# Two output tiles opened at once: the start of the second input product in a two-block kernel

## What is computed

```
x = x + rms_norm(f, norm_ffn_post)            # end of block 1: residual of the feed-forward
h = rms_norm(x, norm1_g_2)                    # start of block 2
z = h @ w_in_2                                # 1024 x 2560: the "second input product"
a, gate, q, k, v = split(z)                   # a, gate: convolution; q, k, v: attention
u = a * sigmoid(gate)                         # then a depthwise convolution with 31 taps
q, k = rms_norm per head; attention over a grid neighbourhood
x = x + concat(conv_out, attn_out) @ w_out_2
```

## Time and profile before

| | us |
|---|---|
| median of 3 runs | 1470.35 (1470.22 to 1470.82) |
| the profiled execution, its own time | 1470.5 |
| its span, from the first instruction recorded to the last | 1468.7 |
| TensorE busy in the span | 1459.0 (99%) |
| VectorE / ScalarE / GpSimd busy | 674.5 / 585.6 / 654.5 |
| the seam: first product of tile 0 starts | 888.01 |
| tile 2 starts | 907.08 |

### The profile page before, as it was taken

One profiled execution on the slowest core, in us unless ns is written; L12 is line 12 of the kernel. 1 busy time (PEld: TensorE's weight loads), 2 busy tenths in 40 slices (PEclk: granted clock), 3 DMA queues, 4 the chain that ended last, 5 costly groups with the idle time before them and its releaser, 6 DMA issues.

```text
span 1468.7 us, 19733 instructions
## 1 busy us (share of the span) xinstructions
PE 1459.0 (99%) x7128; PEld 1179.5 (80%) x7128; DVE 674.5 (46%) x1087; ACT 585.6 (40%) x922; POOL 654.5 (45%) x304
## 2 busy tenths in 40 slices
PE   9999999999999999999999999999999999999999
PEld 7888888888788878888888886777678888888887
DVE  6424755775534286333330108989764333333000
ACT  5143433756553253332232224766654332232221
POOL 4434322762244434444444452766234444444543
PEclk9999999999999999999999999999999999999999
DMA  5433211112123223333233333322122333233333
GB/s 186 147 87 89 84 58 44 58 44 58 58 87 98 89 72 102 99 100 95 90 100 101 113 101 117 112 73 70 42 77 86 100 100 95 91 100 100 100 107 123
DMA packets 38573, 134.15 MB, mean 91 GB/s; under 512 B 4496, under 2 KB 4752, under 8 KB 38512
## 3 DMA queue, kind: packets, MB, share of 16 engines
q1 hardware_dynamic: 37248, 130.70, 29.4%
q10 hardware_dynamic: 1264, 2.62, 0.6%
HBM read 131.20 MB, written 2.10 MB: 91 GB/s over the span
## 4 chain that ended last, share of the span: by engine, by line
PE 78%; issue 13%; DVE 4%; POOL 3%; ACT 0%; DMA 0%; POOLq 0%; SPq 0%; DVEq 0%
PE bank L1157 17%; PE bank L1158 17%; PE bank L1159 17%; POOL wL L483 3%; PE bank L1511 3%; PE bank L1512 2%; PE bank L1513 2%; PE bank L1186 2%; PE bank L1188 2%; PE bank L1187 2%; PE bank L1287 1%; PE bank L1288 1%; PE bank L1289 1%; DVE bank L2247 1%; PE bank L1566 1%
## 5 line engine op out<-in xcount | busy, mean ns | idle before, releaser
L483 POOL TENSOR_TENSOR wL<-raw,wH 128x1024 fp32r<-128x1024 f32 x234 | 574.8, 2457 | 759.5 <-ACT wH L579 621.2
L579 ACT ACTIVATE wH<-raw 128x1024 fp32r<-128x1024 f32 x209 | 221.3, 1059 | 587.3 <-PE bank L1159 519.3
L1157 PE MATMUL bank<-aH,wH 128*128 128x512 f32 x920 | 359.5, 391 | 0.4 <-POOL wL L483 0.3
L1159 PE MATMUL bank<-aH,wL 128*128 128x512 f32 x920 | 358.0, 389 | 0.0
L1158 PE MATMUL bank<-aL,wH 128*128 128x512 f32 x920 | 358.0, 389 | 0.0
L1157 PEld LDWEIGHTS bank<-aH,wH 128*128 128x128 f32 x920 | 172.7, 188 | 38.9 <-issue 1.0
L1159 PEld LDWEIGHTS bank<-aH,wL 128*128 128x128 f32 x920 | 172.7, 188 | 36.1
L1158 PEld LDWEIGHTS bank<-aL,wH 128*128 128x128 f32 x920 | 172.7, 188 | 35.7 <-issue 0.5
L1158 PE MATMUL bank<-fL,wH 128*128 128x512 f32 x352 | 137.0, 389 | 0.0
L1157 PE MATMUL bank<-fH,wH 128*128 128x512 f32 x352 | 137.0, 389 | 0.0
L1159 PE MATMUL bank<-fH,wL 128*128 128x512 f32 x352 | 136.9, 389 | 0.0
(11 more groups left out here) (336 smaller groups left out, 2013.2 us busy)
## 6 DMA issues: line engine op xcount, KB each, us to landing
raw<-in_w SPq DMA_DIRECT2D x234, 512.0 KB, 3.5
bmk<-in_bias SPq DMA_DIRECT2D x6, 512.0 KB, 4.8
out_x<-xT SPq DMA_DIRECT2D x8, 256.0 KB, 4.3
xT<-in_x SPq DMA_DIRECT2D x3, 512.0 KB, 7.3
ct<-in_ct ACTq DMA_DIRECT2D x3, 384.0 KB, 4.0
xT<-in_x SPq DMA_DIRECT2D x2, 256.0 KB, 3.9
raw<-in_w SPq DMA_DIRECT2D x2, 256.0 KB, 4.2
w1k<-in_w1k ACTq DMA_DIRECT2D x1, 512.0 KB, 4.0
```

What stands on the lines that cost most here:

```text
L483: pool.tensor_tensor(wL[:, c_slot, :], raw[:, c_slot, :], wH[:, c_slot, :].bitcast(F32), ALU.subtract).then_inc(sem("w_lo"), 1)
L579: act.activation(wH[:, s, :], raw[:, s, :], ACT.Copy).then_inc(sem("w_hi"), 1)
L1157: pe.matmul(bank[:], hi, H[:, ka, :], start=(k == 0), stop=False)
L1159: mm = pe.matmul(bank[:], lo, H[:, ka, :], start=False, stop=(k == p.k - 1))
```

## The change

At the seam the first two output tiles are worked on together. Five things go with it.

1. The weight stream is laid out anew (`halves_of_two`): the first chunk of `in2` holds k-blocks 0 to 3 of both tiles, the second k-blocks 4 to 7. TensorE does the high products of a k-block for tiles 0 and 1, then the sums, and the low products of k-blocks 0 to 3 in between; those of 4 to 7 come at the end.
2. The sums of squares use `token_sums`: `sq` is the weight (four blocks of 128 tokens), one column of ones the input. The result is 128 tokens x 4 columns.
3. The root is therefore made on 128x4 values (`token_root`), TensorE spreads it over bank 6 after two k-blocks of tile 2, and VectorE copies it to `nr`.
4. VectorE's low parts of k-blocks 0 to 3 lie behind the residuals 2 to 5, the other four at the end.
5. ScalarE converts the chunk of tile 2 between the high parts 5 and 6, and VectorE makes that chunk's low part, which GpSimd made before. `ffn1_done` comes after it.

```diff
@@ -548,7 +548,10 @@
                         .then_inc(sem("conv_add"), 1)
             for t in range(1, NT2 + 1):
-                low((i2 + t + 1) % 2, i2 + t + 2)
+                if t == 2:
+                    pool.wait_ge(sem("w_lo"), i2 + 3)
+                if t > 1:
+                    low((i2 + t + 1) % 2, i2 + t + 2)
                 if 4 <= t < 4 + TAPS // 2:
                     add_taps(2 * t - 7, 2)
             lows(PH["out2"].c0 + 2, NCHUNK)
@@ -949,9 +952,10 @@
             rsqrt(4, narrow(B[4]), D, (sem("sum_ready"), 4), root, narrow(B[5]))
 
-            high_of_x("h3", "g_norm1", "res2", 4, True)
-
             p = PH["in2"]
+            high_of_x("h3", "g_norm1", "res2", 4, True, range(6))
+            ahead(p, 0)
+            high_of_x("h3", "g_norm1", "res2", 4, True, range(6, KD))
             w = PV_AT["dw"] + 3 * TAPS
             def evicted(t):
@@ -1021,7 +1025,7 @@
                 act.wait_ge(sem("na_pv"), TT * (pp + 1))
                 act.activation(rows_first(mH[:, pp, :]), columns_first(B[5][:]), ACT.Copy).then_inc(sem("na_hi"), 1)
-            rsqrt(5, B[6][:], D, (sem("sum_ready"), 5), nr[:], B[5][:])
+            rsqrt(5, narrow(B[6]), D, (sem("sum_ready"), 5), root, narrow(B[5]))
             act.preload_act_table_set("sigmoid_and_others")
             for t in range(1, NT2):
                 kind, n = IN2[t - 1]
@@ -1029,7 +1033,8 @@
                     act.preload_act_table_set("sigmoid_and_others")
                 if t in SPREAD_AT:
                     head_roots_wide(SPREAD_AT[t])
-                ahead(p, t - 1)
+                if t > 1:
+                    ahead(p, t - 1)
                 if t - 1 in VALUES_AT:
                     values(VALUES_AT[t - 1], 1)
                 if kind in "gqk":
@@ -1503,8 +1508,7 @@
             def add_up(k):
                 pe.wait_ge(sem("sq_ready"), 4 * KD + k + 1)
-                pe.matmul(B[6][:], ones, sq[:, k % 2, :], start=(k == 0), stop=(k == KD - 1),
-                          skip_group_check=True).then_inc(sem("sq_used" if k < KD - 1 else "sum_ready"), 1)
+                token_sums(B[6], sq[:, k % 2, :], k == 0, k == KD - 1).then_inc(sem("sq_used" if k < KD - 1 else "sum_ready"), 1)
             def block_product(bank, s, b, H, L, start, stop):
                 hi, lo = wH[:, s, b * P:(b + 1) * P], wL[:, s, b * P:(b + 1) * P]
@@ -1597,38 +1601,39 @@
                 mm.then_inc(sem("na_pv"), 1)
 
-            bank0, bank1 = (B[(p.t0 + t) % NBANK] for t in range(2))
-            s0, s1 = (p.c0 % 2, (p.c0 + 1) % 2)
-            pe.wait_ge(sem("w_lo"), p.c0 + 1)
-            pe.wait_ge(sem("bank_free"), p.t0 + 1)
+            first_two = [B[(p.t0 + t) % NBANK] for t in range(2)]
+
+            def pair_blocks(k):
+
+                return (p.c0 + k // 4) % 2, [slice((t * 4 + k % 4) * P, (t * 4 + k % 4 + 1) * P) for t in range(2)]
+
+            def high_products(k):
+                if k % 4 == 0:
+                    pe.wait_ge(sem("w_lo"), p.c0 + k // 4 + 1)
+                pe.wait_ge(sem("h3_hi"), k + 1)
+                s, blocks_ = pair_blocks(k)
+                for t in range(2):
+                    pe.matmul(first_two[t][:], wH[:, s, blocks_[t]], aH[:, k, :], start=(k == 0), stop=False, skip_group_check=True)
+                    pe.matmul(first_two[t][:], wL[:, s, blocks_[t]], aH[:, k, :], start=False, stop=False, skip_group_check=True)
+
+            def low_products(k):
+                pe.wait_ge(sem("h3_lo"), k + 1)
+                s, blocks_ = pair_blocks(k)
+                for t in range(2):
+                    mm = pe.matmul(first_two[t][:], wH[:, s, blocks_[t]], aL[:, k, :], start=False, stop=(k == KD - 1), skip_group_check=True)
+                if k % 4 == 3:
+                    mm.then_inc(sem("chunk_done"), 1)
+
+            pe.wait_ge(sem("bank_free"), p.t0 + 2)
             for k in range(KD):
-                b = slice(k * P, (k + 1) * P)
-                pe.wait_ge(sem("h3_hi"), k + 1)
-                pe.matmul(bank0[:], wH[:, s0, b], aH[:, k, :], start=(k == 0), stop=False, skip_group_check=True)
-                pe.matmul(bank0[:], wL[:, s0, b], aH[:, k, :], start=False, stop=False, skip_group_check=True)
+                high_products(k)
                 add_up(k)
-            def low_products(ks):
-                for k in ks:
-                    pe.wait_ge(sem("h3_lo"), k + 1)
-                    mm = pe.matmul(bank0[:], wH[:, s0, k * P:(k + 1) * P], aL[:, k, :], start=False, stop=(k == KD - 1), skip_group_check=True)
-                return mm
-
-            def high_products(k):
-                b = slice(k * P, (k + 1) * P)
-                pe.matmul(bank1[:], wH[:, s1, b], aH[:, k, :], start=(k == 0), stop=False, skip_group_check=True)
-                pe.matmul(bank1[:], wL[:, s1, b], aH[:, k, :], start=False, stop=False, skip_group_check=True)
-
-            pe.wait_ge(sem("w_lo"), p.c0 + 2)
-            pe.wait_ge(sem("bank_free"), p.t0 + 2)
-            low_products(range(KD - 3))
-            for k in range(2):
-                high_products(k)
-            low_products(range(KD - 3, KD)).then_inc(sem("chunk_done"), 1)
-            for k in range(KD):
-                if k >= 2:
-                    high_products(k)
-                mm = pe.matmul(bank1[:], wH[:, s1, k * P:(k + 1) * P], aL[:, k, :], start=False, stop=(k == KD - 1), skip_group_check=True)
-            mm.then_inc(sem("chunk_done"), 1)
+                if 2 <= k < 5:
+                    low_products(k - 2)
+                if k == 4:
+                    low_products(3)
+            for k in range(4, KD):
+                low_products(k)
             for t in range(2, NT2):
                 if t >= 4:
                     pe.wait_ge(sem("bank_free"), NBANK + p.t0 + max(t - 1, 1))
@@ -1647,6 +1652,8 @@
                         pe.wait_ge(sem("ln_add"), 3)
                         pe.wait_ge(sem("conv_out"), 3)
                         pe.matmul(B[7][:], ones, ssum[:], start=True, stop=True).then_inc(sem("sum_ready"), 1)
+                    if k == 2 and t == 2:
+                        spread_root(3, B[6])
                     if k == 2 and t in SPREAD_AT:
                         head_spread(SPREAD_AT[t], 0)
                     if k == 3 and t - 1 in STEP_AT:
@@ -1674,7 +1681,7 @@
                     pe.wait_ge(sem("sq_used"), 5 * KD + 4)
                     token_sums(B[7], ssum, True, True).then_inc(sem("sum_ready"), 1)
                 if slot == 20 and b == 3:
-                    spread_root(3, B[7])
+                    spread_root(4, B[7])
                 if slot == 22 and b == 3:
                     value_turns(3, 0)
                 if slot == 23 and b == 2:
@@ -2148,7 +2155,7 @@
             clear_sum(1)
             copy_and_square(PH["out1"], zT, 1)
-            def residual_and_low(src, gain, name, use, next_gain, spread, lows_last=False):
+            def residual_and_low(src, gain, name, use, next_gain, spread, lows):
                 dve.wait_ge(sem("root_spread"), spread)
                 for kt in range(KD):
@@ -2156,13 +2163,12 @@
                         .then_inc(sem(name + "_mul"), 1)
                     dve.wait_ge(sem(name + "_mul"), kt + 1)
                     dve.tensor_tensor(xT[:, kt, :], xT[:, kt, :], tmp[:, kt % 2, :], ALU.add).then_inc(sem(name), 1)
-                    if kt and not lows_last:
-                        low_of_x(use, next_gain, kt - 1)
-                for kt in range(0 if lows_last else KD - 1, KD):
-                    low_of_x(use, next_gain, kt)
+                    for n in lows.get(kt, ()):
+                        low_of_x(use, next_gain, n)
             token_root(2, B[4], D, narrow(B[5]))
-            residual_and_low(zT, "g_mix_post", "res1", "h2", "g_ffn_pre", 1)
+            residual_and_low(zT, "g_mix_post", "res1", "h2", "g_ffn_pre", 1,
+                             {kt: (kt - 1,) if kt < KD - 1 else (kt - 1, kt) for kt in range(1, KD)})
             clear_sum(2)
             for kt in range(KD):
                 add_square(2 * KD + kt)
@@ -2200,17 +2206,23 @@
             clear_sum(3)
             copy_and_square(PH["dn1"], z2T, 3)
             token_root(4, B[4], D, narrow(B[5]))
-            residual_and_low(z2T, "g_ffn_post", "res2", "h3", "g_norm1", 2, True)
+            residual_and_low(z2T, "g_ffn_post", "res2", "h3", "g_norm1", 2,
+                             {2: (0,), 3: (1,), 4: (2,), 5: (3,), KD - 1: range(4, KD)})
+            p = PH["in2"]
+            s_ = (p.c0 + 2) % 2
+            dve.wait_ge(sem("w_hi"), p.c0 + 3)
+            dve.tensor_tensor(wL[:, s_, :], raw[:, s_, :], wH[:, s_, :].bitcast(F32), ALU.subtract).then_inc(sem("w_lo"), 1)
             dve.wait_ge(sem("res2"), KD)
             dve.sem_inc(sem("ffn1_done"), 1)
-            norm(5, B[6], B[5])
+            token_root(5, B[6], D, narrow(B[5]))
+            dve.wait_ge(sem("root_spread"), 3)
+            link(dve.tensor_copy(nr[:], B[6][:]))
```

(10 more changed lines are left out.)

## The result

| | before | changed |
|---|---|---|
| median of 12 runs, us | 1470.14 (1467.99 to 1471.52) | 1473.88 (1470.59 to 1475.38) |
| ratio, 95% interval | | 1.0024 (1.0016 to 1.0032) |
| profiled execution, its own time / span | 1470.5 / 1468.7 | 1474.35 / 1472.6 |

The account below looks back on a forecast made before the run. TensorE, busy 1459.0 of 1468.7 us, was taken as the bound, with VectorE pacing the seam. Seam -0.5, transposes +0.5 and the wait from the held copy +1.2 gave +1.2 us: 1471.6, range 1468.3 to 1474.2.

Parts of the forecast that it names:

- The seam's sum: Seam on TensorE: 18.3 us of work plus 0.2 waiting for high part 6; tile 2 starts 0.5 us earlier.
- spreading the root: Four transposes in tile 2 on TensorE, 0.49 us paid in full: +0.5 us.
- A narrow sum: Four one-column matmuls in the seam take 0.82 us to the next matmul's start, against 0.85 for a wide sum.
- The chunk on VectorE: Tile 2's chunk: its subtraction on VectorE takes 1.3 us, done at 904.3, ahead of tile 2 at 906.6; cost 0.
- The later `ffn1_done`: Behind the seam: it moves from 897.6 to 904.3; GpSimd's zeros and the load for tile 4 still fit; cost 0.
- What VectorE's later `nr` does: Tile 4: copy nrc starts about 0.4 us behind GpSimd's subtraction, is held until 916.3, done 2.6 us later than before.
- How it comes back: Second gating, taps and tile 6's chunk each move by 1.2 us, so TensorE waits 1.2 us ahead of tile 6.
- The clock: TensorE's granted clock: the summed forecast includes no added loss from it; a fall costs about 1.7 us.
- Rival C: Clock falls in the seam behind narrow sums, about 1.7 us each: 1473.3 with one, 1475 with two; chance 0.14.
- A: Rival: the copy nrc is not held and the second gating absorbs VectorE's 0.75 us; 1470.4, no change; chance 0.19.
- D: Rival: the clock fall at 1011 is not repeated, 1.7 us less, 1469.9; chance 0.12.
- B: Rival: the seam's sums are nearly free, tile 2 starts 3.0 us earlier; 1468.6, or 1467.4 without the held copy; chance 0.12.

Follow-up runs that it names:

- run 7: The changed kernel with the low part of tile 2's chunk made by GpSimd again, the copy nrc still from SBUF; ratio 1.0019 to the kernel before.
- run 1: The changed kernel with the copy nrc reading bank 6 instead of nr in SBUF; ratio 1.0003 to the kernel before, median 1470.72 us.
- run 2: The kernel before with one added VectorE pass (bank 6 to a free tile) just ahead of the copy nrc; ratio 1.0015 to the kernel before.
- run 3: The kernel before with the same added VectorE pass as run 2, but just behind the copy nrc; ratio 0.9998 to the kernel before.
- run 5: The changed kernel with wide sums and the root as before, no transposes in tile 2, two tiles still open; ratio 1.0017 to the kernel before.
- run 4: The changed kernel with two unread 512-column matmuls just ahead of TensorE's wait for tile 6's chunk; ratio 1.0009 to the kernel before, median 1471.46 us.
- run 6: Run 5 with nrc made by a second last Newton step reading one SBUF and one bank operand, not copied; ratio 1.0002 to the kernel before.
- run 8: Run 6 with ScalarE converting tile 2's chunk behind high part 7, not ahead of high part 6; ratio 0.9999 to the kernel before.
- run 10: Run 1 with every narrow sum made twice, the first into a bank nobody reads; ratio 1.0111 to the kernel before.
- run 9: Run 1 with seven of the eight sums of squares left out on TensorE; ratio 0.9980 to the kernel before, median 1467.50 us.

## Why the prediction was right, and what it had too small

*The seam's sum* was forecast as 18.6 us and measured as 18.60; *spreading the root* as 0.49 and measured as 0.48. *A narrow sum* was forecast at 0.82 us and took 905.43 - 904.62 = 0.81. The Trainium skill (TensorE: Matmul & The Clock Gate, LDWEIGHTS (loading the stationary operand)) gives 128 columns / 1.2 per load, 107 ns; eight of them would be 0.85 us, an estimate from that figure. The trace roughly agrees, with eight records in 0.81 us. The chunk on VectorE took 1.22 us and cost nothing that can be told (run 7). The later `ffn1_done` cost nothing either; GpSimd's zeros came at 902.97 in the changed kernel's profile, where I had them behind 904.3.

*What VectorE's later `nr` does*: the copy was forecast to start 0.4 us behind GpSimd and started 0.35 behind; it was held, as rows 6 and 7 hinted. That was the step on which the sign rested, and runs 1, 2 and 3 show it from three sides. The two pages of the Trainium skill that the prediction names there (VectorE: DVE Perf Modes, Mode 2×_2P, and GPSIMD Engine Reference, Key points) agree with what the traces show: 2.52 us within SBUF in the changed kernel, 0.68 from a bank in run 1.

*How it comes back* is the mis-sized term: 1.2 us forecast, 1.7 measured. I let ScalarE's taps follow the second gating at once, as they do before. But ScalarE loads a table between its sigmoid and them. Before:

```profile
920.22 1.28 ACT L963 ACT_TABLE_LOAD   x1
922.35 0.82 ACT L1053 ACTIVATE yT<-up,pv 128x512 f32<-128x512 f32 x1 [0.84 <-DVE up L2232]
```

In the changed kernel:

```profile
922.93 0.63 ACT L965 ACTIVATE pk<-pk 128x512 f32<-128x512 f32 x1 [2.89 <-DVE pk L2230]
923.58 1.28 ACT L967 ACT_TABLE_LOAD   x1
924.87 0.81 ACT L1058 ACTIVATE yT<-up,pv 128x512 f32<-128x512 f32 x1
```

Before, the load ended at 921.50 and the taps waited for the gating until 922.35. Now the gating ends at 924.28, as late as forecast (1.2 behind, without the start's 0.75), and the taps wait for the table until 924.87. When the gating got shorter than the load, the load became what is late next: 0.6 us.

*The clock* is the term that the sum put at nothing. Rival C had the mechanism and tied it to the seam. In the changed kernel's profile the clock fell behind the wait ahead of tile 6, which cost 1.4 us. That does not follow from the wait alone: of the four profiles with an idle wait of 1.8 us there, two have the fall (the changed kernel, run 2) and two have not (runs 5 and 7). The clock also fell in the seam in two of the four profiles with eight narrow sums (runs 4 and 7, not the changed kernel and run 1). Of the six profiles with wide sums (before, 2, 3, 5, 6, 8) none has a fall that starts in the seam; in run 3 one started in the window from 885, ahead of it, and reached about half a microsecond into it. Two of four against none of six is no proof that narrow sums at this density cause it; run 10, with twice the density, is strong for it.

How much of the 3.5 us is the clock can be estimated from the mean granted clocks on record. It is 0.9978 over the changed kernel's twelve executions and 0.9991 over the 83 of before that were measured beside the experiments. At the lower level a product takes 0.43 us instead of 0.23, so about half of the time there is lost, and the shares missing from 1.000, times 1470 us, are 3.3 and 1.4 us of loss: about 1.9 us more in the changed kernel. The other 1.6 us fit the +1.73 of the wait. The clocks are recorded to a thousandth, so this is rough. Which wait or which narrow work brings a fall on in a given execution stays open.

A and D did not occur in the changed kernel's profile: the copy was held, and the later fall came again, at 1015. The later fall is absent from the profiles of runs 3, 5, 7, 9 and 10, so it comes and goes whatever the change. B is refuted by runs 9 and 10. Its price of 3 us for free sums was about right: 2.4 in the trace.

So the direction and the path were right, and that the time lies within the range was partly luck. The forecast and the 0.8 us left for the rest end at 1472.4; the range reached 1474.2 only to make room for C, a fall in the seam, and it was used up by the table and by falls that came also elsewhere. The chance of 0.14 for "slower" was too small: C was tied to the seam alone, while the forecast case had a new wait of over a microsecond in it, and rows 10 and 11 had already shown a fall behind narrow work and a wait.

## What to carry to other kernels

Before moving work on VectorE by a few tenths of a microsecond, look which of its instructions read and write only SBUF and what GpSimd does at that moment. The copy here was short when it started first (0.61 us) and lasted until GpSimd was done when it started second (2.52), and reading the same values from a bank avoided it (0.68). Price a sum by a row of the trace and not by its columns: four matmuls of one column, eight records, cost 0.81 us, and one of 512 columns 0.85. And count a new wait of TensorE with the clock that it may cost: here 1.8 us of waiting had a fall of the clock behind it in two profiles of four, worth 1.4 us more in the changed kernel's.

## What was not expected of the hardware

- The holding is one-sided. A copy that started 0.34 us ahead of GpSimd took 0.61 and lengthened GpSimd's 2.40 to 2.54; one that started 0.35 us behind took 2.52 and left GpSimd at 2.40.
- A clock of 0.50 with TensorE shown busy without a gap: run 10, windows from 893 to 903, while one-column matmuls made up more than half of the time.
- A pass with one SBUF and one bank operand, both read in strides, took 1.10 us beside GpSimd (run 6; 1.09 in run 8), between the 0.7 of a free one and the 2.5 of a held one. No run has it beside an idle GpSimd, so whether GpSimd is the cause is not shown.
